# A hybrid decoder block on one core: the layer norm of the second half of the positions applied in the channel layout

## The reference

```python
def layernorm(x, g, b):
    mu = mean(x);  var = mean((x - mu) ** 2)          # over the 512 channels of one position
    return (x - mu) * rsqrt(var + EPS) * g + b

h = rmsnorm(x, g_mix)                                  # x: 1024 positions x 1024
z = h @ w_in;  a, b, v = z[..., :512], z[..., 512:1024], z[..., 1024:]
u = a * sigmoid(b)
u = depthwise_conv(u, conv_w, 31 taps) + conv_b        # causal, per channel
u = silu(layernorm(u, ln_g, ln_b))
q = multiscale_pool(v, pool_w, pool_scale)
x = x + concatenate([u, q]) @ w_out
h = rmsnorm(x, g_ffn);  gu = h @ w_gate_up
x = x + (silu(gu[..., :F]) * gu[..., F:]) @ w_down
gate = sigmoid(rmsnorm(x, g_ple_gate) @ w_ple_gate)
x = x + gate * rmsnorm(p @ w_ple_up, g_ple_post)
return rmsnorm(x, g_final)
```

## Time and profile before

| | us |
|---|---|
| median of three runs | 1003.33 (1003.17 to 1003.41) |
| the profiled execution, device time | 1003.05 |
| its span in the profile | 1001.1 |
| PE busy | 990.6 (99% of the span) |
| PEld busy | 822.1 (82%) |
| DVE busy | 750.3 (75%) |
| ACT busy | 464.0 (46%) |
| POOL busy | 385.3 (38%) |

### The profile page before, as it was taken

The page is one execution under the profiler, slowest core; times in us unless marked ns, Lnnn a source line. Parts: engine busy times, 40 slices in busy tenths (PEclk is TensorE's granted clock), DMA queues, the critical chain, the costliest instruction groups (busy, mean ns, idle before and its releaser), DMA issues.

```text
span 1001.1 us, 12499 instructions
## 1 busy us (share of the span) xinstructions
PE 990.6 (99%) x4543; PEld 822.1 (82%) x4543; DVE 750.3 (75%) x1017; ACT 464.0 (46%) x713; POOL 385.3 (38%) x288
## 2 busy tenths in 40 slices
PE   9999999999999999999999999999999999999996
PEld 7888888888888888888888888888888888888885
DVE  6899999956699575665665665763687888985887
ACT  7635348414363423333333333333444665675775
POOL 3446797710146444444354354451000000011745
PEclk9999999999999999999999999999999999999999
DMA  7421202551224233333332332413998788533222
GB/s 255 152 71 43 85 1 120 205 178 64 105 64 132 80 105 111 100 106 95 116 105 83 127 105 70 141 64 107 359 388 301 232 310 261 196 106 105 85 84 105
DMA packets 103518, 138.25 MB, mean 138 GB/s; under 512 B 6122, under 2 KB 60930, under 8 KB 103458
## 3 DMA queue, kind: packets, MB, share of 16 engines
q1 hardware_dynamic: 103312, 137.20, 40.8%
q10 hardware_dynamic: 146, 0.27, 0.1%
HBM read 104.68 MB, written 32.77 MB: 137 GB/s over the span
## 4 chain that ended last, share of the span: by engine, by line
PE 95%; DVE 2%; issue 1%; ACT 1%; POOL 1%; DMA 0%; POOLq 0%; ACTq 0%; DVEq 0%
PE ps L1552 31%; PE ps L1554 31%; PE ps L1553 31%; PE ps L1606 2%; DVE ftmp L2414 0%; DVE resid L2417 0%; DMA resid<-in_x 0%; DVE spare L1958 0%; ACT junk L975 0%; PE ps L1700 0%; PE ps L1710 0%; ACT act_hi L961 0%; POOL rs L705 0%; PE ps L1690 0%; POOL ss L702 0%
## 5 line engine op out<-in xcount | busy, mean ns | idle before, releaser
L702 POOL TENSOR_SCALAR ss<-ss 128x1 f32<-128x1 f32 x38 | 16.8, 441 | 320.1 <-ACT junk L975 298.8
L2049 DVE SCALAR_TENSOR_TENSOR ps<-resid,convw,ps 128x512 f32<-128x512 f32 x190 | 127.4, 750 | 0.0
L1552 PE MATMUL ps<-ring_hi,ring_lo 128*128 128x512 f32 x308 | 120.0, 390 | 0.1
L1554 PE MATMUL ps<-ring_hi 128*128 128x512 f32 x308 | 119.8, 389 | 0.0
L1553 PE MATMUL ps<-ring_lo,ring_hi 128*128 128x512 f32 x308 | 119.8, 389 | 0.0
L1552 PE MATMUL ps<-act_hi,bs_lo 128*128 128x512 f32 x240 | 93.6, 390 | 0.0
L1554 PE MATMUL ps<-act_hi,bs_hi 128*128 128x512 f32 x240 | 93.4, 389 | 0.0
L1553 PE MATMUL ps<-act_lo,bs_hi 128*128 128x512 f32 x240 | 93.4, 389 | 0.0
L961 ACT ACTIVATE ring_hi<-raw 128x512 fp32r<-128x512 f32 x89 | 51.9, 625 | 60.4 <-PE ps L1554 60.3
L708 POOL TENSOR_TENSOR wc_lo<-raw_b,wc_hi 128x1024 fp32r<-128x1024 f32 x22 | 58.4, 2656 | 48.7 <-ACT wc_hi L961 47.6
L1958 DVE TENSOR_TENSOR ring_lo<-raw,ring_hi 128x512 fp32r<-128x512 f32 x89 | 58.0, 688 | 22.9 <-ACT ring_hi L961 22.7
(11 more groups left out here) (279 smaller groups left out, 2713.7 us busy)
## 6 DMA issues: line engine op xcount, KB each, us to landing
raw<-in_w_gate_up SPq DMA_DIRECT2D x44, 512.0 KB, 5.2
raw<-in_scratch SPq DMA_DIRECT2D x52, 256.0 KB, 3.3
raw<-in_w_down SPq DMA_DIRECT2D x52, 256.0 KB, 4.1
in_scratch<-in_s SPq DMA_DIRECT2D x44, 256.0 KB, 2.7
in_scratch<-gtmp SPq DMA_DIRECT2D x33, 256.0 KB, 2.3
keep<-in_w_down SPq DMA_DIRECT2D x32, 256.0 KB, 4.6
keep<-in_scratch SPq DMA_DIRECT2D x25, 256.0 KB, 3.5
resid<-in_x SPq DMA_DIRECT2D x8, 512.0 KB, 7.0
```

The lines of the kernel that those rows point to most:

```text
L702: pool.tensor_scalar(ss[:, n:n + 1], ss[:, n:n + 1], 1.0 / D, EPS, ALU.mult, ALU.add)\
L1552: pe.matmul(dst, w_lo_, m_hi, start=start, stop=False, skip_group_check=onto)
L1554: return pe.matmul(dst, w_hi_, m_hi, start=False, stop=stop, skip_group_check=onto)
L2049: dve.scalar_tensor_tensor(out=conv_c if k == last_odd else acc, in0=u_all[:, c, k + h * BANK:k + (h + 1) * BANK], scalar=convw[:, c * 32 ...
```

## The change

The second transposition goes for the second half. `conv_turn`, `ln_stats` and POOL's power stay. DVE then writes, per tile, two scaled identity matrices of 128x128 into `diag` (in `scr`): the identity times `lrs`, and the identity times `lrs` times the mean (`ln_diag`). PE multiplies a block of ones (`ones`, in `pw_raw`, filled by POOL) with them, two float32 matmuls with 512 columns: the products hold, on every partition, the row of deviations and the row of means times deviations. They go to PSUM banks 4 and 5. DVE applies them to `conv_o` in the channel layout, per channel block one multiplication and one subtraction in place (`ln_apply`). From there `scale_shift`, `silu`, `mix_high` and `mix_low` work on `conv_o` in SBUF instead of a PSUM bank (`act_place`). The first half keeps its two transpositions.

With it the order changes. `rows_out(3)` is cut: its last 12 matmuls now come behind the two float32 matmuls. `ln_diag` comes behind `add_x(2)`, and the four `ln_apply` between `normed(1, 1)` and `add_x(3)`. At the end of the kernel one addition of 128x1 goes from POOL to ACT.

```diff
+        def act_place(n):
+            h, c = divmod(n, KC)
+            return conv_o[:, c, BANK:2 * BANK] if h else ps[:, SILU_BANK[n], :]
+        diag = scr[:, 2, :].rearrange("p (a s) -> p a s", a=2)
+        ones = pw_raw[:, 0:P]
...
             lo(act_lo[:, 2, BANK:2 * BANK], pw_raw[:, :], act_hi[:, 2, BANK:2 * BANK], pw_lo_ok)
+            pool.wait_ge(pw_lo_ok, 1)
+            pool.memset(ones, 1.0).then_inc(tables_ok, 1)
             window(3)
...
-            pool.wait_ge(ss_ok, 3 * TT + 9)
-            pool.wait_ge(ms_ok, 3 * TT + 7)
-            pool.tensor_scalar(ss[:, n6:n6 + 1], ss[:, p6:p6 + 1], ss[:, n6:n6 + 1], None, ALU.add).then_inc(ms_ok, 1)
             pool.wait_ge(ms_ok, 3 * TT + 9)
             pool.tensor_tensor(rs[:, n6:n6 + 1], ss[:, n6:n6 + 1], neg_half[:, :], ALU.pow).then_inc(rs_ok, 1)
...
             def scale_shift(n):
-                act.wait_ge(lnb_mm, n + 1)
+                if n < KC:
+                    act.wait_ge(lnb_mm, n + 1)
+                else:
+                    act.wait_ge(n_ok, TT + n - KC + 1)
...
+                y = act_place(n)
+                act.activation(sig_place(n), y, ACT.Sigmoid, bias=lnb[:, c:c + 1], scale=lng[:, c:c + 1])
+                act.activation(y, y, ACT.Identity, bias=lnb[:, c:c + 1],
                                scale=lng[:, c:c + 1]).then_inc(y_ok, 1)
...
             square_half(t - 1, C1, 5 * TT, 3 * TT + 9)
+            act.wait_ge(ss_ok, 3 * TT + 9)
+            act.wait_ge(ms_ok, 3 * TT + 8)
+            sum6 = ss[:, 4 * TT - 2:4 * TT - 1]
+            act.activation(sum6, ss[:, 5 * TT:5 * TT + 1], ACT.Identity, bias=sum6).then_inc(ms_ok, 1)
...
-            rows_out(3, range(KD), True, True)
+            out_half(3, 0, range(KD)).then_inc(rows_done, 1)
+            out_half(3, 1, range(4))
             pe.wait_ge(n_ok, TT)
-            for c in range(KC):
-                normed_turn(1, c)
+            pe.wait_ge(tables_ok, N_TABLES + 1)
+            for a in range(2):
+                last = pe.matmul(ps[:, LN_BANK[1][a], :], ones, diag[:, a, :], start=True, stop=True)
+            last.then_inc(lnb_mm, 1)
+            out_half(3, 1, range(4, KD)).then_inc(rows_done, 1)
...
+            def ln_diag(tiles):
+                for t in tiles:
+                    own = slice((t % HT) * P, (t % HT + 1) * P)
+                    dve.wait_ge(lrs_ok, t + 1)
+                    dve.tensor_scalar(diag[:, 0, own], ident[:, :], lrs[:, t:t + 1], None, ALU.mult)
+                    dve.tensor_scalar(diag[:, 1, own], ident[:, :], lrs[:, t:t + 1], mv[:, t, 0:1], ALU.mult, ALU.mult)\
+                       .then_inc(n_ok, 1)
+            def ln_apply(c):
+                y = act_place(KC + c)
+                dve.wait_ge(lnb_mm, KC + 1)
+                dve.tensor_tensor(y, y, ps[:, LN_BANK[1][0], :], ALU.mult).then_inc(bn_ok, 1)
+                dve.wait_ge(bn_ok, TT + c + 1)
+                dve.tensor_tensor(y, y, ps[:, LN_BANK[1][1], :], ALU.subtract).then_inc(n_ok, 1)
...
             ln_stats(range(HT, TT))
-            ln_scale(range(HT, TT))
             add_x(2)
+            ln_diag(range(HT, TT))
             normed(0, 1, 2)
             normed(1, 1, 2)
+            for c in range(KC):
+                ln_apply(c)
             add_x(3)
```

More of the change, by code:

```diff
@@ L950, in _ @@
             pool.tensor_scalar(ss[:, n7:n7 + 1], ss[:, p7:p7 + 1], ss[:, n7:n7 + 1], None, ALU.add).then_inc(ms_ok, 1)
+            pool.wait_ge(ms_ok, 3 * TT + 10)
             pool.wait_ge(ss_ok, 3 * TT + 11)
-            pool.wait_ge(ms_ok, 3 * TT + 10)
             pool.tensor_scalar(ss[:, n7:n7 + 1], ss[:, p7 + 1:p7 + 2], ss[:, n7:n7 + 1], None, ALU.add).then_inc(ms_ok, 1)
@@ L1098, in scale_shift @@
             def scale_shift(n):
-                c, b = n % KC, SILU_BANK[n]
-                act.wait_ge(lnb_mm, n + 1)
+                c = n % KC
+                if n < KC:
+                    act.wait_ge(lnb_mm, n + 1)
+                else:
+                    act.wait_ge(n_ok, TT + n - KC + 1)
                 if n == KC:
                     act.wait_ge(q_lo_ok, GROUPS)
-                act.activation(sig_place(n), ps[:, b, :], ACT.Sigmoid, bias=lnb[:, c:c + 1], scale=lng[:, c:c + 1])
-                act.activation(ps[:, b, :], ps[:, b, :], ACT.Identity, bias=lnb[:, c:c + 1],
+                y = act_place(n)
+                act.activation(sig_place(n), y, ACT.Sigmoid, bias=lnb[:, c:c + 1], scale=lng[:, c:c + 1])
+                act.activation(y, y, ACT.Identity, bias=lnb[:, c:c + 1],
                                scale=lng[:, c:c + 1]).then_inc(y_ok, 1)
@@ L1112, in mix_high @@
                 act.wait_ge(silu_ok, n + 1)
-                copy(act_hi[:, c, h * BANK:(h + 1) * BANK], ps[:, SILU_BANK[n], :], mix_hi_ok)
+                copy(act_hi[:, c, h * BANK:(h + 1) * BANK], act_place(n), mix_hi_ok)
             def evac_e(t):
@@ L1202, in hi_b @@
                 else:
-                    act.wait_ge(lnb_mm, 2 * KC)
+                    act.wait_ge(mix_lo_ok, 2 * KC)
                 dst = bs_hi[:, 2, :] if q % 2 else wa_hi[:, :, :].rearrange("p a s -> p (a s)")
@@ L1799, in _, with out_half @@
             pe.wait_ge(rows_added, 4)
-            rows_out(3, range(KD), True, True)
-            pe.wait_ge(n_ok, TT)
-            for c in range(KC):
-                normed_turn(1, c)
+            def out_half(t, d, ks):
+                c = slice(d * BANK, (d + 1) * BANK)
+                for k in ks:
+                    hi_, lo_, r = wo_stripe(k)
+                    last = product(ps[:, WO_BANK[t] + d, :], act_hi[:, k, t * P:(t + 1) * P],
+                                   act_lo[:, k, t * P:(t + 1) * P], hi_[:, r, c], lo_[:, r, c], k == 0, k == KD - 1)
+                return last
+            out_half(3, 0, range(KD)).then_inc(rows_done, 1)
+            out_half(3, 1, range(4))
+            pe.wait_ge(n_ok, TT)
+            pe.wait_ge(tables_ok, N_TABLES + 1)
[3 more added lines that the diff above has]
+            out_half(3, 1, range(4, KD)).then_inc(rows_done, 1)
             pe.wait_ge(rows_added, 6)
@@ L1819, in _ @@
             pe.wait_ge(rows_added, 12)
[L1820 to L1829, removed]
+            out_half(7, 0, range(KD)).then_inc(rows_done, 1)
+            out_half(7, 1, range(4))
             turn(6, 1)
-            last_half(1, range(4, KD)).then_inc(rows_done, 1)
+            out_half(7, 1, range(4, KD)).then_inc(rows_done, 1)
             def token_half(a, k, odd):
@@ L2076, in ln_scale @@
                                       mv[:, t, 0:1], lrs[:, t:t + 1], ALU.subtract, ALU.mult).then_inc(n_ok, 1)
+            def ln_diag(tiles):
[11 more added lines that the diff above has]
+                dve.tensor_tensor(y, y, ps[:, LN_BANK[1][1], :], ALU.subtract).then_inc(n_ok, 1)
             def silu(n):
-                y = ps[:, SILU_BANK[n], :]
+                y = act_place(n)
                 dve.wait_ge(y_ok, n + 1)
@@ L2086, in mix_low @@
                 dve.wait_ge(mix_hi_ok, n + 1)
-                lo(act_lo[at], ps[:, SILU_BANK[n], :], act_hi[at], mix_lo_ok)
+                lo(act_lo[at], act_place(n), act_hi[at], mix_lo_ok)
             def q_low(s):
@@ L2154, in pair_forms @@
                 if m == 0:
-                    dve.wait_ge(lnb_mm, 2 * KC)
+                    dve.wait_ge(mix_lo_ok, 2 * KC)
                 dve.tensor_tensor(s3[:, :, cols], quarter(0), a21(m), ALU.subtract).then_inc(fs3_ok, 1)
```

## The result

| | before | after |
|---|---|---|
| median us | 1003.37 (1003.05 to 1004.85, 6 runs) | 1008.24 (1006.67 to 1009.64, 6 runs) |
| ratio after to before, 95% interval | | 1.0044 (1.0034 to 1.0054) |
| profiled execution, its span | 1003.05, 1001.1 | 1008.14, 1006.2 |
| PE busy | 990.6 | 992.5 |
| mean granted clock | 0.999 | 0.996 |

The changed kernel is slower by 4.9 us. The sign and the wait were as forecast. The time lies 1.9 us above the 1006.3 of the likeliest case and 0.24 us above the range; it is that of the third rival, the clock, which had got 8%.

A forecast was written before the change was run, and what follows sets the result against it. PE, running back to back, was taken to bound the kernel: 1003.05 + 3.2 (PE's wait) + 0 (its work) - 0.2 (end) = 1006.05, or 1006.3 us with the runs' median 0.28 above. Range for 8 in 10: 1004.8 to 1008.0.

The forecast's parts named there:

- The sign: Whole kernel: slower, by 0.3%; slower by over 0.2% was given 84%.
- the wait: PE ahead of `turn(0, 1)`, for the last `mix_low`: a new wait of about 3.2 us, bounds 2.3 to 3.9.
- the likeliest case: Whole kernel: 1006.3 us, 0.3% slower; the forecast with its own range, 1005.3 to 1007.2, was given 78%.
- the third rival: PE's clock falls during its wait before `turn`, as transposes behind it don't hold it up: 1.85 us, kernel 1008.2; chance 8%.
- PE's own work: Second half on PE: 16 transposes removed (1.75 us), two float32 matmuls added (1.75), net 0; bounds -0.9 to +1.7.
- When PE asks for the diagonals, and whether it waits: Ahead of the two float32 matmuls: diagonals ready at 221.3, PE asks at 224.69, so no wait.
- The chain behind the two matmuls: DVE and ACT: four `ln_apply` take 5.24 us, `add_x(3)` ends at 233.15, last `mix_low` near 243.2.
- The end: Last additions of the kernel, now on ACT: 0.2 us gained, between 0 and 0.25.
- The clock: PE's clock through the wait before `turn`: stays at 1.00, costing nothing; a fall was given 8%.

The follow-up runs named there:

- e3: The changed kernel with ACT's squares of tile 3 moved behind the last high part of the second half: 1004.00 us, ratio 1.0001 to the kernel before.
- e1: The changed kernel with 13 extra, unused matmuls of 512 columns on PE ahead of its wait for the last low part: 1006.97 us, ratio 1.0032 to before.
- e2: The changed kernel with the 24 matmuls of tile 4 put ahead of the 16 transposes behind the wait: 1010.75 us, ratio 1.0062 to before.
- e4: The changed kernel with DVE's `add_x(3)` behind the second of the four `ln_apply` instead of the fourth: 1004.46 us, ratio 1.0006 to before.
- e5: The changed kernel with ACT's squares of tile 3 later and DVE's `add_x(3)` split and moved earlier among the `ln_apply`: 1003.38 us, ratio 0.9999 to before.
- e6: The kernel before with only the last 128x1 addition moved from POOL to ACT: 1003.14 us, ratio 0.9997 to before.
- e7: e5 with four matmuls in the rounded format, high and low parts, instead of the two float32 ones: 1002.80 us, ratio 0.9993 to before.

## Why the prediction was right in its mechanism and short in size

- PE's own work: forecast net 0, measured -0.03 (1.72 for 1.75). Right.
- When PE asks for the diagonals, and whether it waits: no wait; the last diagonal ends at 221.6 in the trace, against a forecast of 221.3. Right.
- The chain behind the two matmuls: eight steps 5.24 forecast, 5.29 measured. `add_x(3)` 233.15 forecast, 233.38 measured, 0.22 of it from the start of the run. From there to the last `mix_low` 10.07 forecast, 9.98 measured; ACT's distance with its source in SBUF is 0.71 (235.18 - 234.47) where I took 0.72. The wait 3.2 forecast, 3.21 measured, and e3 shows that ACT's square in front of `scale_shift(4)` carries it. Right.
- The end: -0.2 forecast, -0.18 measured. Right.
- The clock: this step failed. The sum put it at nothing, because the clock had stayed at 1.00 for 4.6 us of idle PE at the end and "a wait of 3.2 is shorter", and the fall was left 8%. In the profiled execution it cost 1.70 us. One stretch in which the clock held isn't a bound for another. The earlier trace rows stops at 998.00; right behind it, in the same trace, the clock falls:

```profile
998.20:998.50 0.30, 0.00 (x0) 0.00 (x0) 0.00 (x0) 0.00 (x0) 0.00 (x0) 0.82 1.07 403
998.50:998.80 0.30, 0.00 (x0) 0.00 (x0) 0.00 (x0) 0.00 (x0) 0.00 (x0) 0.50 0.91 300
```

  That is 5.3 us behind the end of the last matmul (993.08). The same windows behind the last matmul of the other traces give the fall after 3.6 us (the changed kernel), 3.6 (e1), 3.4 (e2), 2.2 (e3), 5.2 (e4), 4.9 (e5), 3.1 (e6) and 3.5 (e7), with PE idle throughout. The trace of before had the longest of the nine, and a wait of 3.2 us lies inside their spread. In e2 the fall came 2.4 us into the wait.
- The third rival had the event right and its reason wrong. Its reason, that transposes are not enough to hold the clock, isn't needed: in e2 the clock fell before anything had been issued. In the changed kernel it fell half a microsecond into the transposes, and whether other work there would have held it up no run shows. The price, 1.85 us, was 1.70, in part by luck: it was taken from the half speed at the start of the kernel, and there the granted clock isn't low in the rows, so they don't show that stretch to be the lower level:

```profile
2.00:4.00 2.00, 2.00 (x11) 2.00 (x11) 0.00 (x0) 0.58 (x1) 0.00 (x0) 1.00 0.80 287
```

  The Trainium skill (TensorE: Matmul & The Clock Gate, Part 4: PE-mode transpose) says that transposes don't count as busy in the way of matmuls. These runs don't bear that out: in the traces the low stretch was longer with matmuls alone behind the wait (6.8 us) than with 16 transposes first (3.4). They don't refute it either, as the times of single runs fit both lengths in both kernels.

## What to carry to other kernels

On an engine that is the bound, price a new wait as itself plus what it does to TensorE's clock: here 3.2 us of waiting cost 4.9 in the traced run. That the clock held through a longer idle stretch elsewhere in a trace doesn't make a shorter one safe. When work is put in front of an instruction of one engine, look at which engine waits for that instruction in program order for something unrelated; the square of tile 3, whose result DVE takes up at 251.24, over 16 us after it was ready (234.57), held back the whole chain, and moving it gave all but 0.1 us back. A transposition replaced by a float32 matmul saves nothing on TensorE when the matmul goes through twice; the saving is in the rounded format, and it was 0.75 us.

## What the runs showed of the hardware that I had not expected

- With PE idle the clock fell 2.2 to 5.3 us after the end of the last matmul in nine traces, and 2.4 us after it at the wait in e2. In the changed kernel it fell 3.6 us after it, when PE had been at work again for half a microsecond.
- Once down with work behind it, it stayed down for 3.4 us in one trace and 6.8 us in another. What sets the length is open.
- The idle time of 0.4 us in e4 left it at 1.00.
- In the first microseconds of the kernel a transpose record of 128 columns takes 0.23 us where it takes about 0.12 later, while the granted clock in the rows is 1.00. Why is not shown.
